# A tenth place for the experts' weights in the rows of x, in a one-core decoder step

## The reference, cut to what matters

```
h = rmsnorm(x);  u, q, k, v, forget, gates = h @ w_in        # 512 + 3*512 + 8 + 2*1024 columns
pool = windowed means of u through w_pool
att  = softmax attention with forget biases; the sample rows read 8 pages of cached K and V each
x += (sig(g0) * (pool @ w_up_pool) + sig(g1) * (att @ w_up_att)) @ w_out
h = rmsnorm(x);  group = argmax of 4, then the top 2 of its 8 experts, softmax weights
x += sum over 32 experts of ge * ((silu(h @ w_gate[e]) * (h @ w_up[e])) @ w_down[e])
y = rmsnorm(x)
```

## Time and profile before

| | |
|---|---|
| median of 3 runs | 735.04 us (734.88 to 736.56) |
| profiled execution | 734.89 us, its span 733.1 us |
| PE busy | 602.4 us (82%), mean granted clock 0.905 |
| DVE, ACT, POOL busy | 226.0, 83.8, 47.3 us |
| DMA | 269.13 MB, mean 367 GB/s |

### The profile page before, as it was taken

One profiled execution on the slowest core, in us unless ns is written; L12 is line 12 of the kernel. 1 busy time (PEld: TensorE's weight loads), 2 busy tenths in 40 slices (PEclk: granted clock), 3 DMA queues, 4 the chain that ended last, 5 costly groups with the idle time before them and its releaser, 6 DMA issues.

```text
span 733.1 us, 13747 instructions
## 1 busy us (share of the span) xinstructions
PE 602.4 (82%) x6164; PEld 368.6 (50%) x6164; DVE 226.0 (31%) x550; ACT 83.8 (11%) x224; POOL 47.3 (6%) x58
## 2 busy tenths in 40 slices
PE   4899999999999999998667786778767676778774
PEld 3678777775574455554334443344334343444342
DVE  4249689972131462321111111111111111111113
ACT  2211142221101201000000000000000000000003
POOL 4106430112000000000000000000000000000000
PEclk8799999999999999999888898778988898889898
DMA  9967969997999456999999999999999999999992
GB/s 299 301 249 242 251 245 396 295 398 306 414 422 414 169 234 250 426 428 425 422 421 426 427 422 422 427 425 424 425 426 426 424 422 426 425 425 422 424 371 91
DMA packets 36602, 269.13 MB, mean 367 GB/s; under 512 B 5076, under 2 KB 5896, under 8 KB 18103
## 3 DMA queue, kind: packets, MB, share of 16 engines
q1 hardware_dynamic: 29824, 230.91, 78.4%
q0 software_dynamic: 3072, 35.19, 11.9%
q10 hardware_dynamic: 3647, 2.14, 1.0%
HBM read 265.99 MB, written 2.46 MB: 366 GB/s over the span
## 4 chain that ended last, share of the span: by engine, by line
DMA 49%; PE 47%; DVE 1%; ACT 1%; issue 1%; SPq 0%; ACTq 0%; DVEq 0%
DMA ring<-w_up 46%; PE bank L1333 9%; PE bank L1416 8%; PE bank L1508 8%; PE bank L1554 4%; PE bank L1569 4%; DMA wf<-w_in 3%; PE bank L1485 2%; PE bank L1349 1%; PE bank L1316 1%; PE bank L1364 1%; PE bank L1492 1%; PE bank L1369 1%; PE bank L1519 1%; PE bank L1523 1%
## 5 line engine op out<-in xcount | busy, mean ns | idle before, releaser
L1333 PE MATMUL bank<-ring,front 128*32 128x256 f32 x2048 | 163.4, 489 | 100.6 <-DMA ring<-w_up 97.0
L1333 PEld LDWEIGHTS bank<-ring,front 128*32 128x32 f32 x2048 | 89.7, 139 | 166.6 <-issue 142.6
L1192 DVE COPY front<-bank 128x256 f32<-128x256 f32 x32 | 13.6, 425 | 241.7 <-PE bank L1333 241.7
L1349 PE MATMUL bank<-ring,front 128*32 128x256 f32 x1024 | 61.2, 379 | 0.0
L1416 PE MATMUL bank<-hT,ring 128*128 128x264 f32 x256 | 60.9, 398 | 0.0
L1508 PE MATMUL bank<-hT,ring 128*128 128x264 f32 x256 | 59.7, 389 | 0.4 <-ACT front L758 0.4
L1416 PEld LDWEIGHTS bank<-hT,ring 128*128 128x128 f32 x256 | 49.5, 196 | 9.9 <-issue 1.2
L1316 PE MATMUL bank<-front 128*32 128x256 f32 (+1 forms) x768 | 53.0, 390 | 0.3 <-DVE front L1103 0.3
L1508 PEld LDWEIGHTS bank<-hT,ring 128*128 128x128 f32 x256 | 47.8, 190 | 9.7 <-issue 2.1
L815 ACT ACTIVATE front<-bank 128x128 f32<-128x128 f32 x32 | 8.9, 277 | 377.1 <-PE bank L1341 377.1
L1349 PEld LDWEIGHTS bank<-ring,front 128*32 128x32 f32 x1024 | 33.1, 110 | 22.1 <-issue 0.5
(11 more groups left out here) (293 smaller groups left out, 488.2 us busy)
## 6 DMA issues: line engine op xcount, KB each, us to landing
ring<-w_gate SPq DMA_DIRECT2D x31, 2048.0 KB, 33.8
ring<-w_down SPq DMA_DIRECT2D x31, 2048.0 KB, 38.5
ring<-w_up SPq DMA_DIRECT2D x31, 2048.0 KB, 38.3
ring<-w_in SPq DMA_DIRECT2D x8, 2048.0 KB, 22.9
ring<-w_out SPq DMA_DIRECT2D x2, 2048.0 KB, 16.8
front<-q_scratch SPq DMA_DIRECT2D x8, 256.0 KB, 7.8
ring<-w_up_pool SPq DMA_DIRECT2D x1, 2048.0 KB, 30.5
ring<-w_up_att SPq DMA_DIRECT2D x1, 2048.0 KB, 15.7
```

The lines of the kernel that those rows point to most:

```text
L1333: last = m.matmul(bank[GATEUP][32 * g:32 * g + 32, 0:256], xgT[:, k % 2, k // 2], w[:, k, 256 * (g % 2):256 * (g % 2) + 256], start=k == 0 ...
L1349: last = m.matmul(bank[TDOWN][32 * g:32 * g + 32, 0:256], hE[:, j % 2, j // 2], wd[:, j, 256 * g:256 * g + 256], start=j == 0, stop=j == F ...
```

## The change

- x, the sample rows `samp`, the last pooling rows `unew` and the scratch `sqmoe` lie together in a new tensor x9 of 16 KB in each partition. It is a tenth place, free when the residual is in PSUM (s_inj). What shared SBUF with them moves: `samp` and `unew` leave `front`, norm_final goes to free columns of hT, y's rows and the last squares' scratch to a place that no later matrix takes, and three routing temporaries to constants and router weights that are used up.
- The expert matrices are numbered in the order of use (ORDER) and go round all ten places. Matrix n waits for the product that read matrix n - 10. At the end, expert 31's gate and up matrices still come ahead of expert 30's down matrix.
- The broadcasts of the queries 2 to 7 are issued by ScalarE at step `keys` 4(b-1) + 1, on the same condition as before (the products with the query two before are done). The first two stay on SP.
- The step `snew` is split: `sprod`, VectorE's product, is a step behind `nat` of k, and `snew`, the sum and the copy, comes after four `keys` steps. `forgetT` and `bias` come one projection later, and the keys' steps are spread anew.
- ScalarE waits for the prompt's v rows to be written before the second norm.

```diff
-NSLOT = 9
-NB = NSLOT // 3
+RING = 9
+NSLOT = RING + 1
+ORDER = [(e, m) for e in range(LAST - 1) for m in range(3)] + [(LAST - 1, 0), (LAST - 1, 1), (LAST, 0), (LAST, 1), (LAST - 1, 2), (LAST, 2)]
...
+        x9 = sb("x9", [P, SLOT])
+        slot = [ring[:, n * SLOT:(n + 1) * SLOT] for n in range(RING)] + [x9[:]]
...
-        x = sb("x", [P, 3, D])
+        x = x9[:, 0:3 * D].rearrange("p (b n) -> p b n", b=3)
+        samp, unew = x9[:, 3 * D:3 * D + DC], x9[:, 3 * D + DC:4 * D]
+        sqmoe = x9[:, 3 * D:4 * D]
...
-        normf = x[:, 2, :]
-        yst = x[:, 0:2, :]
+        normf = temp(D)
...
-        last_step += [PLAN.index(("pv", CC - 1)), PLAN.index(("merge", DK - 1)), PLAN.index(("merge", DK - 1))]
+        last_step += [PLAN.index(("pv", CC - 1)), PLAN.index(("merge", DK - 1)), PLAN.index(("merge", DK - 1)), PLAN.index(("route", 0))]
+        QROW_AT = 1
         FREED = sorted(range(NSLOT), key=lambda q: last_step[q])
+        home = {item: FREED[n % NSLOT] for n, item in enumerate(ORDER)}
...
-        ready = {("q", b): PLAN.index(("keys", 4 * b - 5)) if b >= 2 else PLAN.index(("nat", C_Q)) for b in range(NS)}
+        ready = {("q", b): PLAN.index(("nat", C_Q)) for b in range(2)}
...
                 else:
-                    sp.wait_ge(s_merge, DK)
-                load_matrix(sp, q // 3, q % 3, q)
+                    sp.wait_ge(s_inj, 1)
+                load_matrix(sp, *ORDER[n], q)
+            def slot_used(n):
+                e, m = ORDER[n - NSLOT]
+                sp.wait_ge(s_gu if m < 2 else s_dn, e + 1)
+            for n in range(NSLOT, len(ORDER)):
+                e, m = ORDER[n]
+                q = home[e, m]
+                slot_used(n)
+                if e < LAST:
+                    load_matrix(sp, e, m, q)
...
+                elif step == "keys" and a % 4 == QROW_AT and a // 4 + 1 in range(2, NS):
+                    b = a // 4 + 1
+                    act.wait_ge(s_kprod, 4 * (b - 1))
+                    act.dma_start(qb[:, b % 2], qd[b].partition_broadcast(P)).then_inc(s_qb[b % 2], 16)
...
-                    elif step == "snew":
+                    elif step == "sprod":
                         dve.wait_ge(*count_taken("proj", C_K, CC - 1))
...
                         ins.then_inc(s_prod2, 1)
+                    elif step == "snew":
```

In PLAN itself, a line of it:

```diff
-PLAN += V[:1] + [("nat", C_K)] + keys(2)[:1] + V[1:2] + [("snew", 0)] + keys(2)[1:2] + V[2:3] + [("scores", 0)] + keys(2)[2:] + V[3:] + [("smax", 0)]
+PLAN += V[:1] + [("nat", C_K), ("sprod", 0)] + keys(2)[:2] + V[1:2] + keys(2)[2:] + [("snew", 0)] + V[2:3] + [("scores", 0)] + keys(3)[:1] + V[3:] + [("smax", 0)]
```

More of the change, by code:

```diff
@@ L126, in sem @@
             return ctx.enter_context(nc.semaphore(name))
-        ring = sb("ring", [P, NSLOT * SLOT + P])
-        slot = [ring[:, n * SLOT:(n + 1) * SLOT] for n in range(NSLOT)]
+        ring = sb("ring", [P, RING * SLOT + P])
+        x9 = sb("x9", [P, SLOT])
+        slot = [ring[:, n * SLOT:(n + 1) * SLOT] for n in range(RING)] + [x9[:]]
         tok = slot[6][:, 0:2 * PB * DC].rearrange("p (i b n) -> p i b n", i=2, b=PB)
@@ L258, in build @@
         ra, em, e1, e2, rr = (temp(3 * 32).rearrange("p (b n) -> p b n", b=3) for _ in range(5))
-        cs, over, ones8 = (temp(256) for _ in range(3))
+        cs, over, ones8 = wre[:].rearrange("p g n -> p (g n)"), wf[:].rearrange("p k n -> p (k n)"), L["mask"]
         r_gm, r_m1, r_m2, r_top, r_gs, r_ts, tex = (temp(3).unsqueeze(2) for _ in range(7))
@@ L479, in load_matrix @@
                 eng.dma_start(slot[q].rearrange("p (g n) -> p g n", g=2), src.rearrange("e (g p c) n -> p (e g) (c n)", g=2, p=P)).then_inc(s_slot[q], 16)
-        LAST = EXPERTS - 1
-        SETS = [len(range(p, LAST, NB)) for p in range(NB)]
         def later_blocks(eng, step):
@@ L543, in _ @@
-            q = 3 * (LAST % NB)
-            sp.wait_ge(s_gu, LAST - NB + 1)
-            for half in range(2):
-                for m in range(2):
-                    src = t[("w_gate", "w_up")[m]][0, LAST].rearrange("(p k) f -> p k f", p=P)
-                    ks = slice(4 * half, 4 * half + 4)
-                    sp.dma_start(slot[q + m].rearrange("p (k n) -> p k n", k=DK)[:, ks], src[:, ks]).then_inc(s_last[2 * half + m], 16)
-            sp.wait_ge(s_dn, LAST - NB)
-            load_matrix(sp, LAST - 1, 2, 3 * ((LAST - 1) % NB) + 2)
@@ new lines, in _ @@
+            for n in range(NSLOT, len(ORDER)):
[4 more added lines that the diff above has]
+                    load_matrix(sp, e, m, q)
+                elif m == 0:
+                    slot_used(n + 1)
+                    for half in range(2):
+                        for gu_half in range(2):
+                            src = t[("w_gate", "w_up")[gu_half]][0, LAST].rearrange("(p k) f -> p k f", p=P)
+                            ks = slice(4 * half, 4 * half + 4)
+                            sp.dma_start(slot[home[LAST, gu_half]].rearrange("p (k n) -> p k n", k=DK)[:, ks], src[:, ks]).then_inc(s_last[2 * half + gu_half], 16)
+                elif m == 2:
+                    src = t["w_down"][0, LAST].rearrange("(g p c) n -> p g c n", g=2, p=P)
+                    for j in range(FC):
+                        sp.dma_start(slot[q].rearrange("p (j n) -> p j n", j=FC)[:, j], src[:, j // 2, j % 2]).then_inc(s_last[4 + j], 16)
@@ L1626, in hidden_gates @@
                 if e < LAST:
[L1627 to L1629 removed]
+                    pe.wait_ge(s_slot[home[e, 0]], arrived[e, 0])
+                    pe.wait_ge(s_slot[home[e, 1]], arrived[e, 1])
+                    gate_up(pair, range(DK)).then_inc(s_gu, 1)
                 else:
@@ L1670, in _ @@
                 pe.wait_ge(s_last[4 + j], 16)
-                last = down(LAST % NB, range(j, j + 1), hLast)
+                last = down(home[LAST, 2], range(j, j + 1), hLast)
             last.then_inc(s_dn, 1)
```

79 lines of the change are left out of this document (33 added, 46 removed).

## The result

| | before | changed |
|---|---|---|
| runs beside each other, us | 734.66, 734.88, 735.04, 736.56 | 727.76, 729.05, 729.07, 729.39 |
| median | 734.96 | 729.06 |
| profiled execution (its span) | 734.89 (733.1) | 727.76 (725.9) |

The ratio is 0.9904, 95% interval 0.9874 to 0.9934: faster by 1.0%. The forecast was 729.7 us. The medians of the same eight runs give 0.9920, inside the range, and the interval holds the forecast's own 0.9927 (5.4 us of 735.04) too. The profiled execution of the changed kernel is also the shortest of its four, by 1.3 us, and I come to the reason.

A forecast was written before the change was run, and what follows sets the result against it. PE was taken to bound the front until expert 0's gate and up product, then DMA of the experts' weights. Terms: -5.0 - 0.67 + 0 + 0.3 = -5.4 us, giving 729.7 us; range 728.2 to 733.0.

The forecast's parts named there:

- (d): First gate weights, loaded later into another place, land just ahead of gate 0: +0.3 us, bounds 0 and 6.1.
- (b): Front: new-token product as its own step removes VectorE's 6.28 us wait, keys run a step ahead; 0 on the path.
- The tenth place: Experts' stretch: one matrix loads in idle DMA time before the first refill; -5.0 us, worth between 0 and 5.05.
- The rival that it buys nothing: Experts' stretch: the tenth load moves only bytes that were hidden, leaving only (a): 734.4 us, chance 0.05.
- (a): Front: forgetT one projection later ends PE's wait for ScalarE's copy; -0.67 us, bounds -0.67 and 0.
- (c): Front: six query broadcasts issued by ScalarE instead of SP cost 0 us, bounds 0 and +1.
- rivals 1 and 2: Waits at gate 0 for its weights: 2.5 us more, 732.2 us, chance 0.22; or 6.1 plus clock 3, 738.5, 0.05.
- rival 2: Gate 0: PE waits 6.1 us for its weights, then a lower clock costs 3 us; 738.5 us, chance 0.05.

The follow-up runs named there:

- experiment 1: Changed kernel, but the first load into x9 waits for expert 0's gate and up product instead of the residual; 734.16 us.
- experiment 2: Changed kernel with the forgetT and bias steps back where they stood before; 729.64 us.
- experiment 3: Kernel before plus the tenth place alone, old order, broadcasts on SP; median 730.91 us, clusters at 729.13 to 731.17 and 733.30 to 737.10.
- experiment 4: Changed kernel (new order) with all query broadcasts on SP again; 729.85 us.
- experiment 11: Tenth place, broadcasts on SP: new order with keys beside the gates at old places, 733.38 us; second kernel, old order with new places, 728.88 us.
- experiment 7: Changed kernel with the second gate weights' load reading the first ones' columns; 730.34 us in one run.
- Experiment 6: Changed kernel with the first gate weights' load also waiting for the second V projection; 729.05 us.
- experiment 10: Old order, tenth place, broadcasts on SP, with the fourth gate weights loaded behind the last query row's broadcast; 735.96 us.
- experiment 5: Changed kernel again, 729.75 us; with first two refills in four pieces each, 729.42; with first half's turned selection written earlier, 727.85; with both edits, 727.49.
- experiment 8: Old order with the tenth place and the query broadcasts on ScalarE; 733.82 us.

## Why the prediction was nearly right in time and too small in size

The forecast was a change of 5.4 us; the ratio and the profiled pair give 7.1, the medians 5.9. With four runs on either side the 0.2 us by which 728.0 misses the range are within what such runs differ by. (The low end itself was worked out from the profiled 734.89; from the 735.04 of the forecast it is 728.3.) Two steps failed all the same. In the runs of the result, all of whose before was in the short cluster, it is (d), priced at +0.3 and measured at 0, and the front's start, for which the sum had nothing: 0.31 us of an earlier first landing and 1.35 us of the clock in the profiled execution. Over many executions it is (b), priced at 0.

**The tenth place**: right. Taken 5.0; the stretch is 5.09 shorter in the traces, and experiment 1 gives 4.8 of it back in its trace and 4.4 to 5.1 in time. The rival that it buys nothing is out. The Trainium skill (DMA: Bandwidth & Descriptors, Specifications) has about 358 GB/s for one core, worked out as half of what the memory stack of two cores gives; with this one core running the trace again does not agree (424 GB/s over 380 us).

**(a) forgetT**: right, -0.67 by the missing wait; the time of experiment 2 is of that size.

**(b) New-token product and the keys' places, priced at 0: the step whose mechanism failed.** The prediction put it so: keys run one step ahead, "PE waits for no key product until 161 us, so this is 0 on the path". That was read from one execution of before, in which the last query row landed 16.3 us after its issue and VectorE waited 1.60 us. TensorE also waits for a key product indirectly, through the normalisation that stands behind the keys in VectorE's queue. In other executions the row lands later, and then VectorE, TensorE and the clock lose 5 to 6 us in a row (experiment 3, one profile of such an execution). On SP's queue the new places issue the row 3 to 5 us earlier, and the long cluster goes (experiments 4, 11). Against the short cluster's median of 735.2 the ten runs of the changed kernel, median 729.3, are 5.9 us faster, against all 84 runs of before, mean 737.5, they are 8.1 faster (mean 729.4): the change is worth over a third more to someone who runs it often than one profile of before tells. (These runs of the changed kernel come from two batches, those of before from five.) That before's long runs have the cause seen in experiment 3's is argued from the same code and the same distance; no profile of before in its long cluster was taken.

That the new-token product itself is worth 0 was right: experiment 11's second kernel has VectorE's 6.28 us wait back and loses nothing.

**(c) The broadcasts on ScalarE**: 0 was right for the new order (experiment 4: 729.85 against 729.06 and 729.75). The bounds of 0 and +1 were wrong in kind: in the old order the same move costs 3.9 us (733.82 against 729.94, the median of experiment 3's short cluster, on another chip), since ScalarE comes to the issue late. I looked at what stands behind a late broadcast on ScalarE and not at who waits for the broadcast.

**(d) The first gate weights**: mis-sized. Taken +0.3, with bounds up to 6.1 and a rival of 2.5 on it; measured 0. I had let the load pass through the 153 GB/s of before's window 74 to 84 us. By experiment 7 such slowness belongs to the bytes of the second gate weights; that it did so in before, where they moved just then, is inferred and not tested. In the changed kernel 74 to 84 us runs at 329 GB/s, and by the bytes of SP's queue the load was in at about 87.5 us, where I had 91.6. Experiment 6 delayed the load by 10.1 us more and TensorE stood 0.65. So rivals 1 and 2 did not come about; rival 2's price for the clock, 3 us, was that of experiment 10 (3.05 us behind a stall of 4.24).

**The clock at the first projection** was not in the sum, and gives the profiled execution 1.35 us over the one before. The range had 1.0 us for the clock, at the end of the kernel. It may explain why that execution is at 727.76 and the other three at 729.05 to 729.39; their traces were not taken. Of the 1.8 us by which experiment 5's profile of the same kernel is later at its first refill, 0.72 are the first projection, 0.31 the first landing and 0.58 the wait for the keys. That one profile pair had all of this on its good side is luck, not part of the change.

The terms as measured are -5.09 - 0.67 + 0 = -5.8 against the forecast's -5.4, and medians of 735.0 and 729.1 give -5.9. The start of the front, 0.31 + 1.35, less the 0.13 and 0.06 lost behind it, makes that the 7.2 of the spans.

## What to carry to other kernels

A margin read from one execution is one draw: where a transfer is waited for by the 1.6 us of [1.60 <-DMA ...] and sits behind 2 MB on the same queue, it may be late in other executions, and an edit that issues it 3 us earlier can be worth more than the one profile says. Ask of a transfer that is moved to another engine when that engine comes to the issue, not only what the queue carries. And where two loads take 10 and 24 us, find out whose bytes are slow before the slow window is laid on a third one.

## What the runs showed of the hardware

- The rate depends on what is read: the second quarter's gate weights came at 159 GB/s, the first quarter's columns in their stead at 364, with the same shape, queue and time (experiment 7, one execution; the first quarter's bytes had been read once before).
- TensorE's clock at a stall: behind 4.24 us it was at 0.52 and 0.62 of 2.4 GHz for the next two windows of 4 us and 16 products took 6.88 us for 3.83; behind 3.38 + 0.66 us it fell to 0.50 too; behind 1.99 + 0.66 us (experiment 8) it stayed at 1.00, and the next 16 products took 3.83.
- A load of 2 MB took 15.2 us when issued at 72.26 us (by the bytes of SP's queue it was in at about 87.5) and 10.2 when issued at 82.39 (experiment 6): 10 us of delay at the issue were 5 at the landing.
- Eight transfers of 0.5 MB in place of two of 2 MB ran at 86 to 330 GB/s for 8 us (276 to 284), where the whole loads had 120 in 278 to 281 and then 418 (experiment 5, one trace each).
